# The last two pairs' sums by halves of the features, the final norm's root begun on ScalarE, and one product by the norm's weights on GpSimd

## The chip, the core and the metric

One core of a Trainium2 chip runs the whole program. A core has TensorE (PE: matrix products into PSUM, the banks `pb0` to `pb7`), VectorE (DVE), ScalarE (ACT), GpSimd (POOL) and SyncE (SP, which here only issues DMAs). The engines run their own instruction streams and meet at semaphores. The metric is the device time of one execution in microseconds (us), lower is better.

## The reference

A first block and a second block of a transformer work on 256 tokens of 1024 features in fp32, and what matters here is the very end of the second block: the hierarchical mixture of experts is added to the residual stream `h`, and one norm over the features follows.

```
def rms_norm(x, g):
    xf = x.astype(jnp.float32)
    y = xf * lax.rsqrt(jnp.mean(xf * xf, axis=-1, keepdims=True) + EPS)
    return (y * g.astype(jnp.float32)).astype(x.dtype)
...
    out = jnp.zeros_like(xn)
    for e in range(N_EXPERTS):
        hid = jax.nn.silu(xn @ w_gate[e]) * (xn @ w_up[e])
        out = out + (hid * cw[..., e:e + 1]) @ w_down[e]
    return out
...
        h = h + hierarchical_moe(rms_norm(h, ffn_norm_g[l]), w_router_group[l], b_router_group[l],
                                 w_router_expert[l], b_router_expert[l],
                                 w_exp_gate[l], w_exp_up[l], w_exp_down[l])
    return rms_norm(h, final_norm_g)
```

There are 32 experts of width 256, of which each token uses two. `EPS` is 1e-6.

## The kernel before

The tokens lie on the 128 partitions in two tiles (t = 0 and 1), the 1024 features beside each other, and a row of 1024 is worked in two halves (h = 0 and 1) of 512, because each PSUM tensor pb is 512 fp32 columns wide. `X` holds the residual stream; `half(X, t, h)` is one 128x512 quarter of it.

The expert stage (the function `sparse`) takes the experts in 16 pairs (`NP` = 16). For a pair p, PE gathers the tokens of the two experts, forms gate and up (line 2363), turns the hidden values (L2371), and multiplies by the down weights into banks 6 and 7 (L2386). ACT copies each half of that result to `YH` rounded to fp32r, the type in which PE multiplies here (L2472), and DVE writes the rest of it to `YL` (L2527). Then `pe_spread` (L2401) brings the pair's rows back to the tokens by a product with the selection matrix `SET`, once with `YH` and once with `YL`, and sums over all pairs in four banks: bank 2t + h for tile t and half h, so pb0 and pb1 belong to tile 0. Eight products a pair: two tiles, two halves, `YH` and `YL`. The eight of pair p - 2 stand in the middle of pair p. For the last two pairs they stand at the end, and the order is by tile: tile 0 of pair 14, tile 0 of pair 15, tile 1 of pair 14, tile 1 of pair 15. Each call of `pe_spread` first waits on the semaphore `yy_lo` for both halves of `YL` of its pair.

`finish` follows. DVE adds each bank to its quarter of `X` (L2551) in the order of (t, h) = (0,0), (0,1), then multiplies one half of tile 0 by the weights `FG` into `S1` (`with_gain`, L2544), and so on again with tile 1's adds and tile 0's other half. ACT squares each quarter and sums the squares (L2555; the sum comes by a second instruction, ACTIVATION_READ_ACCUMULATOR). DVE adds the two half sums of each tile (L2559) and takes the reciprocal root of the two values per partition in `dve_rsqrt` (L1476 to L1496): the value v, m = -v/2, a first guess by a shift and a subtraction on the bits, and three Newton steps, each of two TENSOR_SCALARs on one column (L1490) and one SCALAR_TENSOR_TENSOR (L1496). Then DVE forms tile 1's two halves, X times root times `FG` (L2564), while ACT scales tile 0's two products in `S1` by the root (L2569), and each of the four quarters of the output is stored by a DMA of its own (L2572), three from SP's queue and one from ACT's.

GpSimd does four small memsets of this kernel's own and nothing after 176 us. In the order listings below, pb, YH, YL and SET carry their buffer numbers; YH0/YL0 with SET2 are pair 14, YH1/YL1 with SET3 are pair 15. `s_rs`, `s_step_d`, `s_out_a` and so on are the semaphores; `s_step_d` orders DVE's small steps among themselves. S1 is the output buffer, NR and SM hold small per-partition values.

## Time and profile before

| | us |
|---|---|
| runs shown (3), median | 996.39 |
| lowest and highest | 995.97 and 996.99 |
| the profiled execution, device time | 997.38 |
| its span, first to last instruction | 995.5 |
| PE busy in the span | 970.2 (97%) |
| DVE / ACT / POOL busy | 543.4 / 476.7 / 0.8 |

The profile is of one execution; times in its rows are counted from the first instruction. It is read in three steps: the chain of waits tells what the end of the program hung on, the rows in order of time of one engine tell when each instruction began and how long it took, and the groups by line tell what an instruction of a kind costs. Two consecutive instructions of an engine may overlap by some hundredths of a microsecond, so the step from start to start is often shorter than the duration shown.

### The profile page before, as it was taken

To read this page: it belongs to the slowest core of one execution; us is meant where nothing else is said; L and a number is where in the kernel's file an instruction comes from. 1 tells how busy PE (TensorE), PEld (TensorE's weight loads), DVE (VectorE), ACT (ScalarE), POOL (GpSimd) and SP (SyncE) were. 2 spreads that over 40 slices of the span, in tenths; PEclk is the share of its full clock that TensorE was granted. 3 is DMA by queue.
4 is the path that set the end of the run, shared out by engine and by line. 5 is a ranking of instruction groups with operands and counts; after the bars stand their busy time and mean duration, and the time that the engine had idled before them with its cause. 6 is when DMAs were issued, how large, how long until landed. Compare 5 with 4: busy or idle time off the path is not lost.

```text
span 995.5 us, 13615 instructions
## 1 busy us (share of the span) xinstructions
PE 970.2 (97%) x5479; PEld 743.0 (75%) x5479; DVE 543.4 (55%) x875; ACT 476.7 (48%) x761; POOL 0.8 (0%) x8
## 2 busy tenths in 40 slices
PE   9999999898999999999999999999999999999995
PEld 8879877776889998888889887889874454455442
DVE  5888796655566646555586874676463112112114
ACT  5588555655346344543566656445443222222222
POOL 0000000000000000000000000000000000000000
PEclk9999999999999999999999999999999999999998
DMA  9934465522564555453645735375298999999993
GB/s 299 309 132 170 164 211 170 169 85 86 175 205 149 211 182 199 170 170 129 212 152 167 236 110 170 127 259 170 86 353 283 398 392 394 393 393 395 392 397 118
DMA packets 107268, 223.53 MB, mean 225 GB/s; under 512 B 10185, under 2 KB 15042, under 8 KB 107202
## 3 DMA queue, kind: packets, MB, share of 16 engines
q1 hardware_dynamic: 104752, 219.10, 62.5%
q10 hardware_dynamic: 2450, 3.51, 1.2%
q8 instruction: 46, 0.75, 0.3%
q14 instruction: 20, 0.16, 0.0%
HBM read 221.54 MB, written 1.05 MB: 224 GB/s over the span
## 4 chain that ended last, share of the span: by engine, by line
PE 80%; DVE 9%; ACT 5%; issue 3%; SPq 2%; DMA 1%; ACTq 0%; DVEq 0%
PE pb L461 16%; PE pb L463 16%; PE pb L462 16%; PE pb L2363 11%; PE pb L2386 6%; PE pb L2338 3%; DVE wl L1465 3%; PE pb L2401 3%; ACT wh L934 2%; PE pb L524 2%; DMA raw<-in_w_in 1%; SPq L429 1%; PE pb L595 1%; PE pb L664 1%; PE pb L2312 1%
## 5 line engine op out<-in xcount | busy, mean ns | idle before, releaser
L1465 DVE TENSOR_TENSOR wl<-raw,wh 128x2048 fp32r<-128x2048 f32 (+2 forms) x113 | 248.9, 2209 | 105.8 <-ACT wh L934 105.5
L934 ACT ACTIVATE wh<-raw 128x2048 fp32r<-128x2048 f32 (+2 forms) x114 | 208.3, 1835 | 113.2 <-PE pb L463 104.9
L461 PE MATMUL pb<-wh,th 128*128 128x512 f32 (+2 forms) x620 | 248.5, 401 | 1.3 <-DVE wl L1465 1.3
L463 PE MATMUL pb<-wh,tl 128*128 128x512 f32 (+2 forms) x620 | 242.1, 390 | 0.0
L462 PE MATMUL pb<-wl,th 128*128 128x512 f32 (+2 forms) x620 | 242.0, 390 | 0.0
L461 PE MATMUL pb<-th,wh 128*128 128x256 f32 x544 | 157.2, 289 | 0.2 <-DVE wl L1929 0.2
L463 PE MATMUL pb<-th,wl 128*128 128x256 f32 x544 | 154.1, 283 | 0.0
L462 PE MATMUL pb<-tl,wh 128*128 128x256 f32 x544 | 153.9, 283 | 0.0
L461 PEld LDWEIGHTS pb<-wh,th 128*128 128x128 f32 x620 | 117.1, 189 | 28.9 <-issue 4.1
L463 PEld LDWEIGHTS pb<-wh,tl 128*128 128x128 f32 x620 | 117.1, 189 | 25.7
L462 PEld LDWEIGHTS pb<-wl,th 128*128 128x128 f32 x620 | 117.2, 189 | 22.7
L461 PEld LDWEIGHTS pb<-th,wh 128*128 128x128 f32 x544 | 103.3, 190 | 3.7 <-issue 2.7
L462 PEld LDWEIGHTS pb<-tl,wh 128*128 128x128 f32 x544 | 103.4, 190 | 0.4
L463 PEld LDWEIGHTS pb<-th,wl 128*128 128x128 f32 x544 | 103.2, 190 | 0.0
L2519 DVE SCALAR_TENSOR_TENSOR S<-S,pb 128x256 f32<-128x256 f32 x16 | 6.7, 421 | 146.5 <-ACT S L2463 146.5
L2463 ACT ACTIVATE S<-pb 128x256 f32<-128x256 f32 x16 | 6.1, 383 | 98.2 <-PE pb L2363 98.2
L950 ACT ACTIVATE th<-pb,PC 128x256 fp32r<-128x256 f32 x61 | 25.0, 477 | 41.3 <-PE pb L524 41.3
L2446 ACT ACTIVATE XG<-pb,SM 128x256 f32<-128x256 f32 x64 | 26.6, 471 | 34.5 <-PE pb L2338 32.9
L2527 DVE TENSOR_TENSOR YL<-pb,YH 128x512 fp32r<-128x512 f32 x32 | 22.1, 692 | 34.7 <-ACT YH L2472 34.7
L2472 ACT ACTIVATE YH<-pb 128x512 fp32r<-128x512 f32 x32 | 19.1, 598 | 41.1 <-PE pb L2386 41.1
L2363 PE MATMUL pb<-raw,XG 128*64 128x512 f32 x160 | 36.1, 595 | 0.0
L1520 DVE SCALAR_TENSOR_TENSOR tl<-pb,PC,th 128x256 fp32r<-128x256 f32 x61 | 25.9, 477 | 18.7 <-ACT th L950 18.7
(372 smaller groups left out, 1088.4 us busy)
## 6 DMA issues: line engine op xcount, KB each, us to landing
raw<-in_w_in SPq DMA_DIRECT2D x31, 1024.0 KB, 5.7
raw<-in_w_up SPq DMA_DIRECT2D x16, 1024.0 KB, 6.1
raw<-in_w_down SPq DMA_DIRECT2D x16, 1024.0 KB, 4.9
raw<-in_w_exp_gate SPq DMA_DIRECT2D x20, 512.0 KB, 9.6
raw<-in_w_exp_up SPq DMA_DIRECT2D x20, 512.0 KB, 11.6
raw<-in_w_exp_down SPq DMA_DIRECT2D x10, 1024.0 KB, 13.8
raw<-in_w_xkv SPq DMA_DIRECT2D x8, 1024.0 KB, 5.0
mwh<-in_w_exp_gate SPq DMA_DIRECT2D x14, 512.0 KB, 10.3
```

The source lines that it names most:

```text
L461: PE.matmul(o, lh, rh, start=start, stop=False, skip_group_check=True)
L462: PE.matmul(o, lh, rl, start=False, stop=False, skip_group_check=True)
L463: return PE.matmul(o, ll, rh, start=False, stop=stop, skip_group_check=True)
L934: ACTE.activation(hi_of(i), raw_of(i), ACT.Copy).then_inc(S["hi"], 1)
L950: ACTE.activation(chunk(TH[which], c0 + c), PB[b][:, 0:256], ACT.Copy, scale=col(gain, c) if gain else scale).then_inc(S["turn_hi"], 1)
L1465: DVE.tensor_tensor(lo_of(i), raw_of(i), hi_of(i).bitcast(F), ALU.subtract).then_inc(S["lo"], 1)
L1520: DVE.scalar_tensor_tensor(chunk(TL[which], c0 + c), PB[banks[c % len(banks)]][:, 0:256], col(gain, c) if gain else scale, chunk(TH[which] ...
L2338: m = PE.matmul(b[:, 256 * k:256 * k + 256], l, s[:, t], start=(k == 0 and t == 0 and i == 0), stop=(t == 1 and i == 1), skip_group_check= ...
L2363: m = PE.matmul(b[64 * j:64 * j + 64, :].rearrange("p (g n) -> p g n", g=2), XG[q % 2][:, c + 64 * j:c + 64 * j + 64], w[:, :, j, k], star ...
L2386: m = PE.matmul(PB[6 + h][64 * j:64 * j + 64, :], HT[p % 2][:, 128 * k + 64 * j:128 * k + 64 * j + 64], w[:, j, 512 * h:512 * h + 512], st ...
L2401: m = PE.matmul(PB[2 * t + h][:, :], SET[p % 4][:, 128 * t:128 * t + 128], YY[p % 2][i][:, 512 * h:512 * h + 512], start=(p == 0 and i == ...
L2446: ACTE.activation(chunk(XG[q % 2], 2 * r + k), gather_bank(q, r)[:, 256 * k:256 * k + 256], ACT.Copy, scale=gffn[:, 2 * r + k:2 * r + k + ...
```

## The change

Four edits, all at the end of the expert branch:

1. `pe_spread` loses its argument for the tile. Pair 14 is spread whole (both tiles), and pair 15 by the new `pe_last_spread`: half 0 for both tiles, then half 1 for both tiles, each half behind a wait for its own half of `YL`, and with a signal behind each finished bank.
2. `finish` adds in the order (t, h) = (0,0), (1,0), (0,1), (1,1), one wait per bank, and ACT squares in that order. Tile 0's product by `FG` for half 0 is taken by GpSimd; the one for half 1 stays on DVE, behind all four adds. DVE's and ACT's last scalings both wait for these two products.
3. The root: ACT takes the square root of sum/1024 + EPS of both tiles (`act_seed`), DVE its reciprocal, and one Newton step follows in place of the bit trick and three steps (`dve_rsqrt_seeded`).
4. For it, ACT runs a square root on one column right behind the last pair's turned hidden values, and GpSimd writes EPS to a column at the start, for which DVE's first wait counts to 3.

```diff
@@ pool_main
             POOL.memset(ROW[:, :], 0.0).then_inc(S["zero"], 1)
+            POOL.memset(eps, EPS).then_inc(S["zero"], 1)
...
+        def act_seed(ss, n):
+            ACTE.activation(seed, ss, ACT.Sqrt, bias=eps, scale=1.0 / n).then_inc(S["root"], 1)
+
+        def dve_rsqrt_seeded(dst, ss, n):
+            v, y, t, m = NR[:, 0:2], NR[:, 40:42], NR[:, 80:82], NR[:, 20:22]
+            dve_then(DVE.tensor_scalar(v, ss, 1.0 / n, EPS, ALU.mult, ALU.add))
+            dve_after()
+            dve_then(DVE.tensor_scalar(m, v, -0.5, None, ALU.mult))
+            DVE.wait_ge(S["root"], 1)
+            dve_then(DVE.reciprocal(y, seed))
+            dve_after()
+            for c in range(2):
+                a, g = slice(c, c + 1), y[:, c:c + 1]
+                dve_then(DVE.tensor_scalar(t[:, a], m[:, a], g, g, ALU.mult, ALU.mult))
+            dve_after()
+            DVE.scalar_tensor_tensor(dst, t, 1.5, y, ALU.add, ALU.mult).then_inc(S["rs"], 1)
...
@@ dve_main
-            DVE.wait_ge(S["zero"], 2)
+            DVE.wait_ge(S["zero"], 3)
...
+            def pe_last_spread():
+                p = NP - 1
+                for h in range(2):
+                    PE.wait_ge(S["yy_lo"], 2 * p + h + 1)
+                    for t in range(2):
+                        for i in range(2):
...
+                        m.then_inc(S["spread"], 1)
...
-                for t in range(2):
-                    for p in (NP - 2, NP - 1):
-                        pe_spread(p, (t,))
+                pe_spread(NP - 2)
+                pe_last_spread()
...
@@ act_sparse
                         ACTE.activation(HT[p % 2], rise_bank(p)[:, 0:256], ACT.Copy).then_inc(S["ht"], 1)
+                        if p == NP - 1:
+                            ACTE.activation(seed[:, 0:1], eps, ACT.Sqrt).then_inc(S["const_r"], 1)
...
@@ finish
+            POOL.wait_ge(S["d_fing"], 16)
+            POOL.wait_ge(S["out_x"], 1)
+            POOL.tensor_tensor(half(S1, 0, 0), half(X, 0, 0), FG[:, 0:512], ALU.mult).then_inc(S["out_y"], 1)
+            DVE.wait_ge(S["d_fing"], 16)
+            DVE.wait_ge(S["out_x"], 3)
+            DVE.tensor_tensor(half(S1, 0, 1), half(X, 0, 1), FG[:, 512:1024], ALU.mult).then_inc(S["out_y"], 1)
...
-            dve_rsqrt(fr, [(f2, D)], last="rs")
+            f2_known = steps[0]
+            dve_rsqrt_seeded(fr, f2, D)
             DVE.wait_ge(S["rs"], len(SCALES) + 1)
+            DVE.wait_ge(S["out_y"], 2)
...
+            ACTE.wait_ge(S["step_d"], f2_known)
+            act_seed(f2, D)
             ACTE.wait_ge(S["rs"], len(SCALES) + 1)
+            ACTE.wait_ge(S["out_y"], 2)
             for h in range(2):
-                ACTE.wait_ge(S["out_y"], h + 1)
                 ACTE.activation(half(S1, 0, h), half(S1, 0, h), ACT.Copy, scale=fr[:, 0:1]).then_inc(S["out_a"], 1)
```

PE's last products before the change; the first column is the line, a wait stands in brackets:

```order
L2401 MATMUL pb1<-YL0,SET2 128x512
L2401 MATMUL pb0<-YH1,SET3 128x512 [waits s_yy_lo]
L2401 MATMUL pb0<-YL1,SET3 128x512
L2401 MATMUL pb1<-YH1,SET3 128x512
L2401 MATMUL pb1<-YL1,SET3 128x512
L2401 MATMUL pb2<-YH0,SET2 128x512 [waits s_yy_lo]
L2401 MATMUL pb2<-YL0,SET2 128x512
L2401 MATMUL pb3<-YH0,SET2 128x512
L2401 MATMUL pb3<-YL0,SET2 128x512
L2401 MATMUL pb2<-YH1,SET3 128x512 [waits s_yy_lo]
L2401 MATMUL pb2<-YL1,SET3 128x512
L2401 MATMUL pb3<-YH1,SET3 128x512
```

And with the change (L2422 is `pe_spread`, L2433 `pe_last_spread`):

```order
L2422 MATMUL pb1<-YL0,SET2 128x512
L2422 MATMUL pb2<-YH0,SET2 128x512
L2422 MATMUL pb2<-YL0,SET2 128x512
L2422 MATMUL pb3<-YH0,SET2 128x512
L2422 MATMUL pb3<-YL0,SET2 128x512
L2433 MATMUL pb0<-YH1,SET3 128x512 [waits s_yy_lo]
L2433 MATMUL pb0<-YL1,SET3 128x512
L2433 MATMUL pb2<-YH1,SET3 128x512
L2433 MATMUL pb2<-YL1,SET3 128x512
L2433 MATMUL pb1<-YH1,SET3 128x512 [waits s_yy_lo]
L2433 MATMUL pb1<-YL1,SET3 128x512
L2433 MATMUL pb3<-YH1,SET3 128x512
```

Pair 15's products of half 0 for both tiles now come before those of half 1, and all of pair 14 before them; before, the first product of pair 15 waited for both halves of its `YL`, now it waits for the first half, and only the products of half 1 wait for the second.

DVE at the end before the change, from the first add to the last scaling:

```order
L2551 TENSOR_TENSOR X<-X,pb 128x512 [waits s_spread,s_d_fing]
L2551 TENSOR_TENSOR X<-X,pb 128x512
L2544 TENSOR_TENSOR S<-X,FG 128x512 [waits s_out_x]
L2551 TENSOR_TENSOR X<-X,pb 128x512 [waits s_spread]
L2551 TENSOR_TENSOR X<-X,pb 128x512
L2544 TENSOR_TENSOR S<-X,FG 128x512 [waits s_out_x]
L2559 TENSOR_TENSOR NR<-NR 128x2 [waits s_out_a]
L1476 TENSOR_SCALAR NR<-NR 128x2 [waits s_step_d]
L1480 TENSOR_SCALAR NR<-NR 128x2 [waits s_step_d]
L1481 TENSOR_SCALAR NR<-NR 128x2
L1483 TENSOR_SCALAR NR<-NR 128x2 [waits s_step_d]
L1490 TENSOR_SCALAR NR<-NR 128x1 [waits s_step_d]
```

And with the change:

```order
L2578 TENSOR_TENSOR X<-X,pb 128x512 [waits s_spread] x4
L2590 TENSOR_TENSOR S<-X,FG 128x512 [waits s_out_x,s_d_fing]
L2593 TENSOR_TENSOR NR<-NR 128x2 [waits s_out_a]
L1511 TENSOR_SCALAR NR<-NR 128x2 [waits s_step_d]
L1513 TENSOR_SCALAR NR<-NR 128x2 [waits s_step_d]
L1515 RECIPROCAL NR<-SM 128x2 [waits s_root]
L1519 TENSOR_SCALAR NR<-NR 128x1 [waits s_step_d]
L1519 TENSOR_SCALAR NR<-NR 128x1
L1521 SCALAR_TENSOR_TENSOR NR<-NR 128x2 [waits s_step_d]
L2600 SCALAR_TENSOR_TENSOR S<-X,NR,FG 128x512 [waits s_out_y,s_rs]
```

One of DVE's two products by `FG` is gone and the other stands behind the adds; between the sum of the squares and the scaling there are six small instructions where there were thirteen.

ACT before the change, from the last turned hidden values on:

```order
L2483 ACTIVATE S<-pb 128x256 [waits s_used,s_ht_mm]
L2472 ACTIVATE YH<-pb 128x512 [waits s_spread,s_down_mm]
L2472 ACTIVATE YH<-pb 128x512 [waits s_spread,s_used]
L2555 ACTIVATE S,NR<-X 128x512 [waits s_out_x] x4
L2569 ACTIVATE S<-S,NR 128x512 [waits s_out_y,s_rs]
L2569 ACTIVATE S<-S,NR 128x512 [waits s_out_y]
```

And with the change:

```order
L2513 ACTIVATE S<-pb 128x256 [waits s_used,s_ht_mm]
L2515 ACT_TABLE_LOAD
L2515 ACTIVATE SM<-SM 128x1
L2502 ACTIVATE YH<-pb 128x512 [waits s_spread,s_down_mm]
L2502 ACTIVATE YH<-pb 128x512 [waits s_spread,s_used]
L2583 ACTIVATE S,NR<-X 128x512 [waits s_out_x] x4
L1506 ACTIVATE SM<-NR,SM 128x2 [waits s_step_d]
L2607 ACTIVATE S<-S,NR 128x512 [waits s_out_y,s_rs]
```

A table load and a square root of one column stand behind the turned hidden values, and one square root stands behind the four squares; no further table load stands in this branch.

GpSimd before the change has no instruction of its own in the expert branch. With it, from the memsets of the start on (L2587 is the product in `finish`):

```order
L1448 MEMSET RA 128x8x3
L1450 MEMSET BT 128x4x16 [waits s_turn_lo]
L2774 TENSOR_LOAD KW [waits s_flag]
L2782 COMPARE_AND_BRANCH
L2587 ISA
L2587 TENSOR_TENSOR S<-X,FG 128x512 [waits s_out_x,s_d_fing]
L2782 UNCONDITIONAL_BRANCH
```

## Rows read from the trace of the kernel before

**Rows 1.** By stretch: busy us of each engine (instructions), clock, DMA share, GB/s.

```profile
743.00:750.00 7.00, 6.21 (x38) 4.29 (x38) 6.70 (x18) 2.22 (x7) 0.00 (x0) 1.00 0.51 186
...
780.00:960.00 180.00, 180.00 (x922) 88.13 (x920) 34.80 (x84) 45.88 (x109) 0.00 (x0) 1.00 1.04 393
```

**Rows 2.** The chain that ended last, in order of time: start us, us, what.

```profile
981.16 0.70 DVE YL L2527
...
983.22 1.28 DVE X L2551 x2
...
987.11 0.17 DVE NR L2559
...
990.04 0.07 DVE S L2564
```

**Rows 3.** In order of time, PE: start us, us, engine, line, operation [idle before].

```profile
980.75 0.39 PE L2401 MATMUL pb<-YL,SET 128*128 128x512 f32 x1
980.98 0.39 PE L2401 MATMUL pb<-YH,SET 128*128 128x512 f32 x1
...
981.91 0.50 PE L2401 MATMUL pb<-YH,SET 128*128 128x512 f32 x1 [0.30 <-DVE YL L2527]
...
982.71 0.40 PE L2401 MATMUL pb<-YL,SET 128*128 128x512 f32 x1
```

**Rows 4.** In order of time, DVE, from the last pair to the root.

```profile
980.30 0.69 DVE L2527 TENSOR_TENSOR YL<-pb,YH 128x512 fp32r<-128x512 f32 x1 [4.27 <-ACT YH L2472]
...
984.42 0.69 DVE L2544 TENSOR_TENSOR S<-X,FG 128x512 f32<-128x512 f32 x1
...
987.30 0.17 DVE L1476 TENSOR_SCALAR NR<-NR 128x2 f32<-128x2 f32 x1
987.51 0.17 DVE L1480 TENSOR_SCALAR NR<-NR 128x2 f32<-128x2 f32 x1
...
987.98 0.46 DVE L1490 TENSOR_SCALAR NR<-NR 128x1 f32<-128x1 f32 x2
988.47 0.16 DVE L1496 SCALAR_TENSOR_TENSOR NR<-NR 128x2 f32<-128x2 f32 x1
```

**Rows 5.** In order of time, ACT, the last pair and the squares.

```profile
979.67 0.60 ACT L2472 ACTIVATE YH<-pb 128x512 fp32r<-128x512 f32 x1 [4.09 <-PE pb L2386]
...
983.95 0.63 ACT L2555 ACTIVATE S<-X 128x512 f32<-128x512 f32 x1 [2.82 <-DVE X L2551]
...
984.58 0.62 ACT L2555 ACTIVATE S<-X 128x512 f32<-128x512 f32 x1
...
986.37 0.61 ACT L2555 ACTIVATE S<-X 128x512 f32<-128x512 f32 x1
```

**Rows 6.** In order of time, all engines: a hand-over from DVE to ACT.

```profile
742.04 0.16 DVE L1880 TENSOR_TENSOR KW<-KW 128x8 f32<-128x8 f32 x1
742.22 0.20 ACT L1437 ACTIVATE KW<-KW 128x8 f32<-128x8 f32 x1
```

**Rows 7.** By line, ACT, shapes apart: busy us, mean ns, idle before.

```profile
L950 ACT ACTIVATE th<-pb,PC 128x256 fp32r<-128x256 f32 x61 | 25.0, 477 | 41.3 <-PE pb L524 41.3
...
L950 ACT ACTIVATE th<-pb 128x256 fp32r<-128x256 f32 x18 | 5.5, 389 | 12.0 <-PE pb L524 12.0
```

**Rows 8.** One line each, durations min/median/max in ns: L1782, then L1005.

```profile
L1782 DVE RECIPROCAL SM<-SM x4: 158/163/166, 687.7 to 707.7; 128x2 f32<-128x2 f32 x4
...
L1005 ACT ACT_TABLE_LOAD  x1: 1283/1283/1283, 98.3 to 98.3; - x1
```

**Rows 9.** In order of time, POOL at the start.

```profile
0.73 0.31 POOL L1444 MEMSET ROW<- 128x256 f32 x1 [0.29 <-POOLq L2755]
```

**Rows 10.** In order of time, PE weight loads: the last wait for a transfer.

```profile
972.60 0.32 PEld L2386 LDWEIGHTS pb<-BT,S 128*64 128x64 f32 x4 [0.54 <-DMA BT<-in_w_exp_down]
```

**Rows 11.** DMA issues: tensor, queue, KB each, us to landing; stretch 985 to 996.

```profile
out<-S SPq DMA_DIRECT2D x3, 256.0 KB, 2.9
```

**Rows 12.** The page, DMA issues of the whole span.

```profile
raw<-in_w_exp_gate SPq DMA_DIRECT2D x20, 512.0 KB, 9.6
```

More of the change, by code:

```diff
@@ L148 @@
      "sel", "cs_w", "ch_mm", "ch", "g_mm", "g_x", "rise_t", "rise_g", "over_mm", "ht_mm", "ht", "down_mm", "yy_hi", "yy_lo", "spread",
-     "xt_sum", "h_weighted", "out_x", "out_a", "out_y"])
+     "xt_sum", "h_weighted", "out_x", "out_a", "out_y", "root"])
 SEQ = S
@@ L270, in build @@
         rsx, hrsx = small(2), small(2)
+        eps, seed = small(1), small(2)
         hb, sp4, sp4n, sp8n = small(16), small(8), small(8), small(8)
@@ L2391, in pe_down, with pe_spread @@
                             m.then_inc(S["down_mm"], 1)
-            def pe_spread(p, tiles=(0, 1)):
+            def pe_spread(p):
                 PE.wait_ge(S["yy_lo"], 2 * p + 2)
@@ L2397, in pe_spread @@
                     PE.wait_ge(*gathered(0, 3))
-                for t in tiles:
+                for t in range(2):
                     for h in range(2):
@@ L2401, in pe_spread @@
                             m = PE.matmul(PB[2 * t + h][:, :], SET[p % 4][:, 128 * t:128 * t + 128], YY[p % 2][i][:, 512 * h:512 * h + 512],
-                                          start=(p == 0 and i == 0), stop=(p == NP - 1 and i == 1), skip_group_check=True)
-                if len(tiles) == 2 or p == NP - 1:
-                    m.then_inc(S["spread"], 1)
+                                          start=(p == 0 and i == 0), stop=False, skip_group_check=True)
+                m.then_inc(S["spread"], 1)
[3 more added lines that the diff above has]
+                    PE.wait_ge(S["yy_lo"], 2 * p + h + 1)
+                    for t in range(2):
+                        for i in range(2):
+                            m = PE.matmul(PB[2 * t + h][:, :], SET[p % 4][:, 128 * t:128 * t + 128], YY[p % 2][i][:, 512 * h:512 * h + 512],
+                                          start=False, stop=(i == 1), skip_group_check=True)
+                        m.then_inc(S["spread"], 1)
             def pe_sparse():
@@ L2533, in sparse @@
             dve_sparse()
-            finish(FG, [(S["spread"], NP - 1), (S["spread"], NP)])
+            finish(FG, [(S["spread"], NP + n) for n in range(4)])
         fs, fr, f2 = NR[:, 120:124], NR[:, 124:126], NR[:, 126:128]
         def finish(FG, done):
-            def with_gain(h):
-                DVE.wait_ge(S["out_x"], h + 1)
-                DVE.tensor_tensor(half(S1, 0, h), half(X, 0, h), FG[:, 512 * h:512 * h + 512], ALU.mult).then_inc(S["out_y"], 1)
-            DVE.wait_ge(S["d_fing"], 16)
-            for t in range(2):
-                DVE.wait_ge(*done[t])
-                for h in range(2):
+            for h in range(2):
+                for t in range(2):
+                    DVE.wait_ge(*done[2 * h + t])
                     o = half(X, t, h)
                     DVE.tensor_tensor(o, o, PB[2 * t + h][:, :], ALU.add).then_inc(S["out_x"], 1)
-                with_gain(t)
-            for j in range(4):
-                ACTE.wait_ge(S["out_x"], j + 1)
-                ACTE.activation(S0[:, 512 * j:512 * j + 512], half(X, j // 2, j % 2), ACT.Square,
-                                accum_out=fs[:, j:j + 1]).then_inc(S["out_a"], 1)
+            for n in range(4):
+                h, t = n // 2, n % 2
+                j = 2 * t + h
+                ACTE.wait_ge(S["out_x"], n + 1)
+                ACTE.activation(S0[:, 512 * j:512 * j + 512], half(X, t, h), ACT.Square,
+                                accum_out=fs[:, j:j + 1]).then_inc(S["out_a"], 1)
+            POOL.wait_ge(S["d_fing"], 16)
[4 more added lines that the diff above has]
+            DVE.tensor_tensor(half(S1, 0, 1), half(X, 0, 1), FG[:, 512:1024], ALU.mult).then_inc(S["out_y"], 1)
             s4 = fs.rearrange("p (t b) -> p t b", t=2)
@@ L2716, in dense @@
             dve_dense()
-            finish(FG, [(S["used"], NU)] * 2)
+            finish(FG, [(S["used"], NU)] * 4)
         early.close()
```

## Prediction

> **What bounds the kernel now.** I read the stretches first, then the chain of waits, then each engine in order of time. In the long expert stage PE is busy for all of 180 us from 780 to 960 while DVE and ACT work 35 and 46 us of it [rows 1]. So nothing that the change touches is worth anything before PE's last pair is done; it is the tail after it that can move. The chain runs there [rows 2] through DVE's second `YL` (981.16), PE's last spreads, the adds (983.22), the squares on ACT (the last at 986.37, [rows 5]), the sum of the squares (987.11) and DVE's small steps to the root, used at 990.04. From there to the end of the span at 995.5 lie the two scalings and the four stores; the change leaves these as they are, so what reaches 990.04 earlier ends the program earlier by as much. One figure is to be worked out: when is the root ready?
>
> **PE and the first add.** Now PE stops once: after four products it waits for the second `YL` and restarts at 981.91 [rows 3]. The products step by 0.23 us (980.75 to 980.98). With the change all eight of pair 14 run first, and by then `YL` of pair 15 is long there: its first half ends at 980.30 + 0.69 = 980.99 [rows 4], its second at 981.86 [rows 2]. So product n starts at 980.75 + (n - 2) x 0.233, and the stop (about 0.47 us against that step) is gone. But the first add does not wait for eight products any more, it waits for ten, since pair 14's tile 1 comes first: the tenth starts at 982.61. Today the eighth starts at 982.71 and the add 0.51 us later [rows 2, 3]; so the first add starts at 983.12, only **0.10 us** earlier. The next banks are finished by products 12, 14 and 16, ready for DVE at 983.59, 984.05 and 984.52.
>
> **The adds and squares.** Two adds take 1.20 us from start to start (983.22 to 984.42, [rows 2, 4]), 0.60 each. Four in a row start at 983.12, 983.72, 984.32 and 984.92; no bank is late for them, so the adds are DVE's pace. Before, a product by `FG` (0.69 us long, one more step of about 0.60) stood between adds two and three. ACT starts the first square 0.73 us after the first add's start (983.22 to 983.95) and steps by 0.63 (983.95 to 984.58) [rows 5]: 983.85, 984.48, 985.11, 985.74. The fourth add's result is there at 984.92 + 0.73 = 985.65, so ACT's own pace decides by a little. The sum of the squares starts 0.74 us after the last square's start (986.37 to 987.11), at **986.48** against 987.11: 0.63 us won. DVE's remaining product by `FG` starts at 984.92 + 0.60 = 985.52 and ends at 986.21, under ACT's last square, so it costs nothing; if that cover went, it would cost up to its 0.69.
>
> **The root.** Before: 987.11 to 990.04, 2.93 us [rows 2]. After, counted from the sum's start: the sum takes 0.16 and is followed by both ACT's square root and DVE's v. A hand-over of a small result from DVE to ACT costs 0.02 (742.04 + 0.16 to 742.22), and a small function takes 0.20 there [rows 6]. No row shows a square root of two columns whose bias is a column in memory; the nearest bound of what that column adds is 477 - 389 = 88 ns, the same instruction with and without a column as operand [rows 7]. I take 0.29; the ends are 0.20 and, were a table load to stand in front, 0.29 + 1.28 [rows 8]. So the square root is ready at 0.18 + 0.29 = 0.47, with a hand-over of 0.03 at 0.50. DVE's v starts at 0.19, m at 0.19 + 0.21 = 0.40 (987.30 to 987.51, [rows 4]), and m's step ends sooner than 0.50 allows, so ACT decides by a few hundredths. The reciprocal takes 0.16 (four rows of that shape, [rows 8]) plus 0.03 to the next dependent step: 0.69. The two column steps lead to the last step in 0.49 (987.98 to 988.47), which takes 0.16 + 0.03: **1.37 us**. The root is ready at 986.48 + 1.37 = 987.85, against 990.04.
>
> **The load of the tables and the small additions.** ACT's new table load and one-column root stand behind the last hidden values; 1.28 + 0.20 = 1.5 us, and ACT sits idle there for 4.09 us before 979.67 [rows 5]. It costs nothing; without that gap it would cost 1.5 us. The later squares and copies need no other load: the listing of ACT shows none. EPS in a column is one more small memset beside one of 0.31 us that starts at 0.73 us [rows 9], long before DVE's first use; it costs nothing for the same reason. On PE, DVE and ACT nothing else in the program moves; the late wait of both scalings for the two products of `FG` asks only that GpSimd is done.
>
> **The product on GpSimd.** The trace has no product there, only memsets. Its lower bound is DVE's own 0.69. From a memset of 256 columns in 0.31 [rows 9], 512 columns would be about 0.6 for a single stream, and three streams (two read, one written) one after the other some 1.4 to 1.8 us: my estimate is 1.4. It starts when the first add is done, about 983.12 + 0.70 = 983.82, and ends at about 985.2. It is needed at 987.85: a cover of 4.0 us. It costs nothing at either bound. The Trainium skill (GPSIMD Engine Reference, section Elementwise side-by-side cycle accounting) states 4497 ns for a product of this kind on 2048 columns; a quarter of that is an estimate of 1.1 us, and the sum would stay the same.
>
> **The sum.** 0.63 + (2.93 - 1.37) = 0.63 + 1.56 = 2.19 us. The profiled execution would go from a span of 995.5 to 993.3 and from 997.4 to 995.2; the median of the runs, 996.39, lies 1.0 below that execution, and the difference of the two kernels holds for both: **994.2 us**. That is 0.22%. A difference under 0.2% (2.0 us) is about what a measurement of this kernel cannot tell from none, so the forecast lies just beyond that line, and every tenth counts.
>
> **Rival 1: GpSimd and DVE get in each other's way.** GpSimd reads `X` and `FG` in just the time in which DVE does adds three and four. Nothing in the trace speaks for or against, since the two never work side by side there. If DVE's adds stood still while GpSimd works, the third add would start at 985.2 in place of 984.32, the fourth at 985.8, its square at 986.53 and the sum at 987.27: the 0.63 becomes -0.16, the gain 1.40 and the time 995.0. The Trainium skill (SBUF — State Buffer, the part on the shared port pair) says that a DVE instruction with two inputs in SBUF blocks and is blocked by one of GpSimd that reads SBUF, but not one with a single such input. By that rule the adds, whose other input is PSUM, are free, and only DVE's product would stand behind GpSimd's, from the point where that takes over 1.7 us (985.52 - 983.82); no run here shows it yet. Chance 0.14.
>
> **Rival 2: GpSimd's code is not there, slower than before.** The change brings the first real work on GpSimd, and with it a load of its code, at the head of the branch and without a wait in front. If this is done at once (about 744 us) it has 239 us of cover. It may add bytes to the weight stream, which fills the queues from 780 to 960 and at 972.60 keeps PE waiting 0.54 us [rows 1, 10]; but from 743 to 750 the queues are only half busy, so I count 0. If instead the code is fetched when the product is first run, at 983.9, the scalings wait for it. Everything is as before where fetch and product take 6.2 us (983.82 to 990.04), and the kernel is slower by over 0.2% from 8.2 us on. The price of a fetch is bounded by a 256 KB transfer on empty queues, 2.9 us [rows 11], and 512 KB on loaded ones, 9.6 us [rows 12]. With 2.9 + 1.4 the root waits 0.3 us (994.5); with 9.6 + 1.4 the end moves by 4.8 us, to 1001.2, and this is the rival. The listing has the load far in front, which speaks against it. The Trainium skill (GPSIMD Engine Reference, section Instruction dispatch) gives about 6 us for the first call after a load; were that paid at the product, by an estimate the time would be 997.6. Chance 0.05, of which 0.03 above 0.2%.
>
> **Rival 3: the steps are there but each costs a little more.** Hand-overs between ACT and DVE that are 0.05 to 0.1 longer, or a root of 0.4, cost 0.2 to 0.4 us: 994.4 to 994.6. That is the forecast's own case, on the other side of the line. I give forecast and this 0.78 together, split 0.57 beyond 0.2% and 0.21 within. That leaves 0.03 for things unseen, such as a further table load behind the first (1.28 us, time 995.5), all within 0.2%.
>
> **Chances and range.** Faster by over 0.2%: 0.57. Slower by over 0.2%: 0.03. Within: 0.21 + 0.14 + 0.02 + 0.03 = 0.40. The range goes from 993.3 (the sum is 0.3 us short, and the runs' own spread of half a microsecond) to 995.5, which takes in rival 1 and the table load; above it lies rival 2.
>
> **What will show it.** PE's last 16 products without a stop; the first add at about 983.1, no idle time between the four adds; the sum of the squares at about 986.5; a square root of about 0.29 us on ACT right behind it, no table load after 979; the scaling at about 987.9 and 1.4 us after the sum; GpSimd's product of 0.7 to 1.8 us beginning at 983.8. Adds that take longer than 0.69 us or that leave gaps would show rival 1; a scaling that waits for GpSimd, rival 2. The prediction is wrong if the tail after the root does not keep its 5.5 us.

## The result and the profile after

| | before | changed |
|---|---|---|
| median of 16 runs, us | 996.67 | 994.86 |
| lowest and highest | 995.64 and 998.36 | 993.17 and 996.83 |
| the profiled execution's span | 995.5 | 991.5 |
| in it: first of PE's last 16 spread products | 980.42 | 978.61 |
| in it: the root's first use | 990.04 | 985.96 |
| the tail between the two | 9.62 | 7.35 |

The ratio of the runs is 0.9977, with a 95% interval of 0.9970 to 0.9984: 2.3 us faster, or between 1.6 and 3.0. The medians differ by 1.8 us. The forecast of 994.2 us, 2.19 us faster, lies 0.7 us below the measured median and inside the interval of the difference; whether the gain passes 0.2% the interval leaves open.

The end of the chain of waits of the changed kernel, in order of time (start us, us, what), answers to [rows 2]:

```profile
978.68 2.06 PE pb L2422 x8
980.74 0.47 PE pb L2433 x2
...
981.24 0.70 DVE X L2578
...
981.96 2.57 ACT S L2583 x8
...
984.55 0.17 DVE NR L2593
...
985.96 0.07 DVE S L2600
```

PE's last products stand in it as one run without a stop, the four squares and their sums as one run of 2.57 us, and 1.41 us lie between the sum (984.55) and the root's use (985.96), where there were 2.93.

The same stretch of the changed kernel by instructions, in order of time, for DVE, ACT and GpSimd, answers to [rows 4, 5]:

```profile
981.24 2.48 DVE L2578 TENSOR_TENSOR X<-X,pb 128x512 f32<-128x512 f32 x4 [1.19 <-PE pb L2433]
...
981.96 0.63 ACT L2583 ACTIVATE S<-X 128x512 f32<-128x512 f32 x1 [2.63 <-DVE X L2578]
...
982.08 1.29 POOL L2587 TENSOR_TENSOR S<-X,FG 128x512 f32<-128x512 f32 x1 [806.36 <-DVE X L2578]
...
983.20 0.61 ACT L2583 ACTIVATE S<-X 128x512 f32<-128x512 f32 x1
983.64 0.68 DVE L2590 TENSOR_TENSOR S<-X,FG 128x512 f32<-128x512 f32 x1
...
983.81 0.61 ACT L2583 ACTIVATE S<-X 128x512 f32<-128x512 f32 x1
...
984.55 0.16 DVE L2593 TENSOR_TENSOR NR<-NR 128x2 f32<-128x2 f32 x1 [0.23 <-ACT S L2583]
...
984.75 0.30 ACT L1506 ACTIVATE SM<-NR,SM 128x2 f32<-128x2 f32 x1 [0.23 <-DVE NR L2593]
...
985.08 0.17 DVE L1515 RECIPROCAL NR<-SM 128x2 f32<-128x2 f32 x1
985.28 0.46 DVE L1519 TENSOR_SCALAR NR<-NR 128x1 f32<-128x1 f32 x2
985.77 0.16 DVE L1521 SCALAR_TENSOR_TENSOR NR<-NR 128x2 f32<-128x2 f32 x1
```

The four adds take 2.48 us as one run, in steps of 0.60; GpSimd's product works from 982.08 to 983.37 beside them; DVE's own product ends at 984.32, while ACT is still at its last square. The square root starts at the same time as DVE's v (984.75), takes 0.30 us, and the reciprocal follows 0.03 us behind it. And before it, the load of ACT's tables in its gap:

```profile
973.80 1.28 ACT L2515 ACT_TABLE_LOAD   x1
...
975.09 0.20 ACT L2515 ACTIVATE SM<-SM 128x1 f32<-128x1 f32 x1
...
977.87 0.60 ACT L2502 ACTIVATE YH<-pb 128x512 fp32r<-128x512 f32 x1 [2.58 <-PE pb L2407]
```

The load and the one-column root are over at 975.29, 2.58 us before ACT's next work, which answers to the 4.09 us of idle time in [rows 5].

One thing in the two spans is not of the change. The tail became 2.27 us shorter, the span 4.0. The other 1.8 us lie before the tail: PE's last products began at 978.61 in place of 980.42. The start of each of PE's 5479 products compared between the two traces shows where: the kernel before is 0.4 us behind from 127 us on (it leaves that for a few us around 184 and 208 and comes back), 1.9 from 234 us on, and stays between 1.7 and 1.95 behind from there to the tail (1.80 at its start). Between 229 and 233 us PE's granted clock was down in the one execution and not in the other. Rows by stretch, the columns as in [rows 1], of the kernel before:

```profile
229.00:231.00 2.00, 2.00 (x10) 1.71 (x10) 1.90 (x5) 1.61 (x3) 0.00 (x0) 0.65 0.96 374
```

and of the changed kernel:

```profile
229.00:231.00 2.00, 2.00 (x11) 1.67 (x10) 1.57 (x4) 1.97 (x3) 0.00 (x0) 1.00 1.05 409
```

The granted clock was 0.65 of full speed on average in one and full in the other. So what the change is worth is read from the tail, and the whole time is compared by many runs only.

### The profile page after: what moved, and what is told of

Same layout as the page of the kernel before. It is cut to its first block, busy times and chain, and to the rows that moved or that the text cites. A ratio compares the mean times of both kernels' runs of the same rounds, so it can differ in the third digit from the quotient of the medians.

```text
span 991.5 us, 13616 instructions
## 1 busy us (share of the span) xinstructions
PE 970.7 (98%) x5479; PEld 744.8 (75%) x5479; DVE 541.4 (55%) x867; ACT 478.0 (48%) x764; POOL 2.1 (0%) x10
## 4 chain that ended last, share of the span: by engine, by line
PE 81%; DVE 8%; ACT 5%; issue 3%; SPq 2%; DMA 1%; ACTq 0%; DVEq 0%
PE pb L462 17%; PE pb L464 16%; PE pb L463 16%; PE pb L2384 11%; PE pb L2407 6%; PE pb L2359 3%; PE pb L2422 3%; DVE wl L1467 3%; ACT wh L935 2%; PE pb L525 2%; PE pb L596 1%; SPq L430 1%; DMA raw<-in_w_in 1%; PE pb L665 1%; PE pb L2333 1%
```

## The experiments

All tails below are measured in the profiled execution of each kernel, from the first of PE's last 16 spread products to the first use of the root (start of DVE's first scaling), so what happened earlier in that execution does not enter. The time from there to the end of the span was 5.4 to 5.6 us in all twelve traces.

| kernel | expected tail | measured tail | of which up to the sum of the squares |
|---|---|---|---|
| before | | 9.62 | 6.69 |
| changed | 7.43 (forecast) | 7.35 | 5.94 |
| e1, root alone | 8.11 | 8.09 | 6.68 |
| e2, all but the root | 8.87 | 8.87 | 5.94 |
| e3, both products on DVE | 7.75 | 7.63 | 6.22 |
| e4, order by tiles | 8.1 | 8.09 | 6.68 |
| e5, 1024 columns on GpSimd | 7.35 or 8.5 | 8.30 | 6.02, and it stood for 1.03 |
| e6, no early load | 8.4 | 8.45 | 5.95 |
| e7, no Newton step | 6.66 | 6.74 | 5.95 |
| e8, half 0 first | 6.98 | 6.92 | 5.50 |
| e10, e8 and e7 | 6.3 | 6.30 | 5.50 |
| e11, e7 with v and m | 6.68 or 6.74 | 6.67 | 5.94 |

### e1: the new root alone

```diff
 (the kernel before)
-            dve_rsqrt(fr, [(f2, D)], last="rs")
+            f2_known = steps[0]
+            dve_rsqrt_seeded(fr, f2, D)
...
+            ACTE.wait_ge(S["step_d"], f2_known)
+            act_seed(f2, D)
```

> The kernel before with the new root alone (square root on ACT, reciprocal and one Newton step on DVE, table load behind the last hidden values); orders and products as before. Measure: the tail, from the first of PE's last 16 spread products to the first use of the root, 9.63 us before and 7.35 us with the whole change. Theory (the savings are separate steps of one chain and add up): the stretch from the sum of the squares to the use of the root is 1.41 us in place of 2.93, so the tail is 8.11 us and the time 1.5 us under the kernel before. Rival (what one part frees, the other would have hidden): less than 1.2 us won here.

Measured: the sum starts 6.68 us into the tail as before, the root is used 1.41 us behind it, the tail is 8.09. The time is 995.3 us, median of 12 runs, against 995.8 for 23 of the kernel before; ratio 0.9992 (0.9981 to 1.0004). The expected 0.9985 lies in that interval, which also holds no gain at all: the whole time alone would not have shown this step, the trace does. The rival of a hidden root falls.

### e2: everything but the root

```diff
-            f2_known = steps[0]
-            dve_rsqrt_seeded(fr, f2, D)
+            dve_rsqrt(fr, [(f2, D)], last="rs")
...
-            ACTE.wait_ge(S["step_d"], f2_known)
-            act_seed(f2, D)
...
-                        if p == NP - 1:
-                            ACTE.activation(seed[:, 0:1], eps, ACT.Sqrt).then_inc(S["const_r"], 1)
```

> The changed kernel with the old root (bit trick and three Newton steps on DVE, no square root and no table load on ACT); the new order of PE, adds and squares and the product on GpSimd stay. Theory (steps add up): the sum of the squares starts 5.94 us after the first spread product as in the changed kernel, the root takes 2.93 us, the tail is 8.87 us and the time about 0.7 us under the kernel before, which 5 rounds can hardly tell from none. Rival: if the order brings something only together with the new root, the tail is 9.4 us or more.

Measured: sum at 5.94, root 2.93 behind it, tail 8.87, all three as expected. Time 996.25 us against 995.8, ratio 1.0001 (0.9992 to 1.0011): the 0.75 us that the trace shows lie at the edge of what these runs can tell. 9.62 - 8.09 = 1.53 for the root and 9.62 - 8.87 = 0.75 for the rest make 2.28, and the whole change gave 2.27. The two parts add up; neither needs the other.

### e3: both products by the weights on DVE

```diff
-            POOL.wait_ge(S["d_fing"], 16)
-            POOL.wait_ge(S["out_x"], 1)
-            POOL.tensor_tensor(half(S1, 0, 0), half(X, 0, 0), FG[:, 0:512], ALU.mult).then_inc(S["out_y"], 1)
             DVE.wait_ge(S["d_fing"], 16)
             DVE.wait_ge(S["out_x"], 3)
+            DVE.tensor_tensor(half(S1, 0, 0), half(X, 0, 0), FG[:, 0:512], ALU.mult).then_inc(S["out_y"], 1)
```

> The changed kernel with both products by the norm's weights on DVE, behind the four adds; GpSimd does nothing at the end. Theory (GpSimd's part is to keep DVE free before the sum): the products start 5.03 and 5.63 us after the first spread product, the second ends at 6.32, the sum starts at 6.34 in place of 5.94 and the tail is 7.75 us, 0.4 more than with the change. Rival (GpSimd's product slows something that is now free of it): the adds or squares get shorter than 0.60 and 0.61 us a step, and the tail is under 7.6 us.

In order of time, DVE and ACT in e3:

```profile
983.35 0.68 DVE L2587 TENSOR_TENSOR S<-X,FG 128x512 f32<-128x512 f32 x1
...
983.95 0.68 DVE L2588 TENSOR_TENSOR S<-X,FG 128x512 f32<-128x512 f32 x1
984.05 0.19 ACT L2583 ACTIVATION_READ_ACCUMULATOR S<-X 128x1 f32 x1
984.55 0.15 DVE L2591 TENSOR_TENSOR NR<-NR 128x2 f32<-128x2 f32 x1
```

The second product starts at 983.95 and holds the sum of the squares, which ACT had ready at 984.24, until 984.55: 0.28 us later than in the changed kernel, not the 0.40 that I had expected (the second product let the sum start 0.60 behind its own start, where I had counted 0.71). Adds and squares keep their steps, so the rival falls. GpSimd's product is worth 0.28 us.

### e4: the order by tiles

```diff
-                pe_spread(NP - 2)
-                pe_last_spread()
+                for t in range(2):
+                    for p in (NP - 2, NP - 1):
+                        PE.wait_ge(S["yy_lo"], 2 * p + 2)
...
-            for h in range(2):
-                for t in range(2):
-                    DVE.wait_ge(*done[2 * h + t])
+            for t in range(2):
+                DVE.wait_ge(*done[t])
+                for h in range(2):
```

> The changed kernel with the order by tiles back, in PE's last spreads, the adds and the squares; GpSimd's product and the new root stay. Theory (the gain ahead of the root is that of the order): PE stops for the second remainder again, tile 1's banks are both finished only behind the 16th product, the third add starts 4.67 us after the first product, the sum at 6.7 and the tail is 8.1 us, 0.75 more than with the change. Rival (the gain ahead of the root comes from the product taken off DVE): the third add starts before 4.4 and the tail is under 7.7 us.

In order of time, DVE and GpSimd in e4 (the tail starts at 980.76):

```profile
983.48 1.28 DVE L2584 TENSOR_TENSOR X<-X,pb 128x512 f32<-128x512 f32 x2 [1.28 <-PE pb L2463]
...
984.32 1.29 POOL L2593 TENSOR_TENSOR S<-X,FG 128x512 f32<-128x512 f32 x1 [806.35 <-DVE X L2584]
...
985.35 1.29 DVE L2584 TENSOR_TENSOR X<-X,pb 128x512 f32<-128x512 f32 x2 [0.59 <-PE pb L2463]
...
987.44 0.16 DVE L2599 TENSOR_TENSOR NR<-NR 128x2 f32<-128x2 f32 x1 [0.20 <-ACT S L2589]
```

The third add starts 4.59 us into the tail, though DVE had been free since 984.76: it waits for tile 1's banks. The sum starts at 6.68, the place that it had before the change, with GpSimd's product in place and DVE relieved. So the product alone wins nothing. The order wins the 0.74 us ahead of the root, of which 0.28 depends on the product being off DVE.

e4 brings two things back at once, PE's stop and the finishing by tiles, and no run parts them. An estimate from rows of the changed kernel: with all of pair 14 first but pair 15 by tiles, tile 0's banks would both be finished by the 12th product (981.27, 2.66 us into the tail), the first add would start 0.43 behind it, and the sum 3.31 behind that as in the changed kernel, at 6.40. By this about 0.3 us of the 0.74 belong to the stop and somewhat over 0.4 to the order by halves.

### e5: the two engines side by side

```diff
-            POOL.wait_ge(S["out_x"], 1)
-            POOL.tensor_tensor(half(S1, 0, 0), half(X, 0, 0), FG[:, 0:512], ALU.mult).then_inc(S["out_y"], 1)
+            POOL.wait_ge(S["out_x"], 3)
+            POOL.tensor_tensor(S1[:, 0:1024], X[:, 0:1024], FG[:, 0:1024], ALU.mult).then_inc(S["out_y"], 2)
             DVE.wait_ge(S["d_fing"], 16)
-            DVE.wait_ge(S["out_x"], 3)
-            DVE.tensor_tensor(half(S1, 0, 1), half(X, 0, 1), FG[:, 512:1024], ALU.mult).then_inc(S["out_y"], 1)
```

> The changed kernel, but GpSimd takes both halves of tile 0 by the norm's weights in one product of 1024 columns behind the third add, and DVE none. GpSimd then works from about 4.6 to 7.1 us after the first spread product, while DVE does the small steps of the root, of which the sum of the squares and the last step read two inputs in SBUF. Theory A (the two engines do not hinder each other on these): the sum starts at 5.94 and the tail is 7.35 us, or as long as GpSimd needs if that is later. Theory B (an instruction of DVE with two SBUF inputs stands until GpSimd's is done): the sum starts only at about 7.1 and the tail is 8.5 us.

In order of time, GpSimd, ACT and DVE in e5:

```profile
985.69 2.34 POOL L2587 TENSOR_TENSOR S<-X,FG 128x1024 f32<-128x1024 f32 x1 [809.37 <-DVE X L2578]
...
986.73 0.19 ACT L2583 ACTIVATION_READ_ACCUMULATOR S<-X 128x1 f32 x1
987.02 1.03 DVE L2591 TENSOR_TENSOR NR<-NR 128x2 f32<-128x2 f32 x1 [0.91 <-ACT S L2583]
988.09 0.17 DVE L1511 TENSOR_SCALAR NR<-NR 128x2 f32<-128x2 f32 x1
```

DVE's sum of two pairs of numbers, 0.15 or 0.16 us long in every other trace, takes 1.03 us and ends at 988.05; GpSimd's product ends at 988.03. Theory B holds: an instruction of DVE that reads two inputs in SBUF stood until GpSimd was done. DVE's fourth add, which reads one input in SBUF and one in PSUM, began at about 985.4 and so ran on beside the product from 985.69; in the changed kernel adds two to four run beside GpSimd in their steps of 0.60. The Trainium skill (SBUF — State Buffer, Who interferes with whom) states that a DVE instruction with two SBUF inputs contends with a GpSimd instruction that reads SBUF, and one with at most one SBUF input does not; the measurement agrees. The tail is 0.95 us longer than with the change, in place of the 1.15 expected, since the sum ends when GpSimd is done, where I had counted it to start then. The sum's start is 0.08 us later than with the change (6.02 against 5.94); that has another cause, told under e7.

### e6: the table load where nothing hides it

```diff
-                        if p == NP - 1:
-                            ACTE.activation(seed[:, 0:1], eps, ACT.Sqrt).then_inc(S["const_r"], 1)
```

> The changed kernel without the one-column square root behind the last hidden values, so that the table load falls behind the four squares. Theory (the load costs its 1.28 us where nothing hides it, and starts when ACT's last square is read): the square root starts 1.06 us later than with the change, 7.2 us after the first spread product, and the tail is 8.4 us. Rival (a switch of tables costs more than the load shows): the tail is 9 us or more. Rival 2 (the load can run ahead of the squares): under 7.6 us.

In order of time, ACT and DVE in e6:

```profile
984.71 0.19 ACT L2581 ACTIVATION_READ_ACCUMULATOR S<-X 128x1 f32 x1
984.92 1.28 ACT L1506 ACT_TABLE_LOAD   x1
...
986.21 0.30 ACT L1506 ACTIVATE SM<-NR,SM 128x2 f32<-128x2 f32 x1
986.54 0.17 DVE L1515 RECIPROCAL NR<-SM 128x2 f32<-128x2 f32 x1 [1.04 <-ACT SM L1506]
```

The load starts 0.02 us behind ACT's read of the last sum and takes 1.28, the square root follows 0.01 later. The tail is 8.45, 1.10 more than with the change: less than the load's duration, since it starts beside DVE's sum of the squares and does not wait for it. So this load costs no more than its own duration; the Trainium skill (ScalarE: Activation LUTs, What ACT_TABLE_LOAD costs) adds a drain of 1380 ns to it, which this run does not show: between the read of the last sum (ended at 984.90) and the square root there is nothing but the load. Putting it behind the last hidden values kept 1.1 of the 1.5 us that the new root wins.

### e7 and e11: no Newton step

```diff
 (e7)
-            dve_then(DVE.tensor_scalar(v, ss, 1.0 / n, EPS, ALU.mult, ALU.add))
-            dve_after()
-            dve_then(DVE.tensor_scalar(m, v, -0.5, None, ALU.mult))
             DVE.wait_ge(S["root"], 1)
-            dve_then(DVE.reciprocal(y, seed))
-            dve_after()
-            for c in range(2):
...
-            dve_after()
-            DVE.scalar_tensor_tensor(dst, t, 1.5, y, ALU.add, ALU.mult).then_inc(S["rs"], 1)
+            DVE.reciprocal(dst, seed).then_inc(S["rs"], 1)
```

> The changed kernel without the Newton step: the root is the reciprocal of ACT's square root as it is, so the value of the norm is less exact. Theory (ACT's square root sets the start of the reciprocal, DVE's two preparing steps ran beside it): the reciprocal starts 0.53 us behind the sum of the squares as in the changed kernel, and the scaling 0.19 later, so the tail is 6.66 us, 0.69 less. Rival (the two preparing steps held the reciprocal back): it starts 0.1 or more earlier, tail under 6.6 us.

In order of time, e7:

```profile
985.26 0.30 ACT L1506 ACTIVATE SM<-NR,SM 128x2 f32<-128x2 f32 x1 [0.23 <-DVE NR L2583]
985.66 0.17 DVE L1511 RECIPROCAL NR<-SM 128x2 f32<-128x2 f32 x1 [0.44 <-ACT SM L1506]
```

The tail is 6.74, 0.61 less than with the change where 0.69 had been expected. The reciprocal starts 0.10 us behind the end of the square root, where it is 0.03 in the changed kernel. e11 keeps DVE's two preparing steps in front of it, though nothing uses them:

> e7_no_newton, but DVE still computes v and m, which nothing uses, between the sum of the squares and the reciprocal; the Newton step is left out. In e7 the reciprocal started 0.10 us behind the end of the square root, in the changed kernel 0.03. Theory A (the hand-over is quicker where DVE has just run another step): the reciprocal starts 0.53 us behind the sum, the tail is 6.68 us. Theory B (it is not, the 0.07 belongs to the way the two instructions meet in that run): 0.59, tail 6.74 us as in e7.

```profile
984.83 0.30 ACT L1506 ACTIVATE SM<-NR,SM 128x2 f32<-128x2 f32 x1 [0.23 <-DVE NR L2587]
...
985.03 0.17 DVE L1513 TENSOR_SCALAR NR<-NR 128x2 f32<-128x2 f32 x1
985.15 0.17 DVE L1515 RECIPROCAL NR<-SM 128x2 f32<-128x2 f32 x1
...
985.36 1.42 DVE L2594 SCALAR_TENSOR_TENSOR S<-X,NR,FG 128x512 f32<-128x512 f32 x2
```

The square root ends at 985.13, the reciprocal starts at 985.15, and the tail is 6.67. Two steps more on DVE made the chain 0.07 us shorter, the number of theory A. But that DVE had just run another step is not the reason: in e6 the hand-over was 0.03 too, after DVE had been idle for 1.04 us. The kernels differ in the waits in front of the reciprocal. In the changed kernel, e6 and e11, DVE's wait for the step before stands ahead of v, and the reciprocal has only the wait for the square root. In e7 and e10 v is gone, and both waits stand in front of the reciprocal. The chain of waits of e7 shows the wait for the square root (L1510) as a piece of its own on DVE's queue, between the end of the square root (985.56) and the reciprocal (985.66):

```profile
985.60 0.02 DVEq L1510
```

e10 has the same piece and 0.10 us. So has the sum of the squares in e5: its kernel leaves out DVE's product, so that the waits for `FG` and for the squares both stand in front of the sum, which starts 0.10 us behind ACT in place of 0.03:

```profile
986.96 0.02 DVEq L2590
```

In all of these, and in the first add of the kernel before (below), the wait that has the piece is the second in the code and the last to be met. The changed kernel's last scalings have two waits too, but there the one that is met last stands first, and they start 0.03 us behind the root without such a piece. That the order of two waits decides it fits every row; no run swaps them.

### e8 and e10: another order of the last products

```diff
 (e8)
-                pe_spread(NP - 2)
-                pe_last_spread()
+                two(a, 0, 0)
+                two(a, 0, 1)
+                PE.wait_ge(S["yy_lo"], 2 * b + 1)
+                two(b, 0, 0).then_inc(S["spread"], 1)
+                two(b, 0, 1).then_inc(S["spread"], 1)
+                two(a, 1, 0)
+                PE.wait_ge(S["yy_lo"], 2 * b + 2)
+                two(b, 1, 0).then_inc(S["spread"], 1)
+                two(a, 1, 1)
+                two(b, 1, 1).then_inc(S["spread"], 1)
```

`two(p, h, t)` stands for the two products of pair p, half h, tile t; a is pair 14, b pair 15.

> The changed kernel with another order of PE's last 16 products: pair 14 for half 0, pair 15 for half 0, then bank by bank for half 1, so that the four banks are finished behind products 6, 8, 12 and 16 in place of 10, 12, 14 and 16. Theory (after the change, the chain hangs on the first bank and four squares of 0.61 behind it; with earlier banks it hangs on the 16th product): the first add starts 1.7 us after the first product, the fourth at 4.1, the sum at 5.57, the tail is 6.98 us, 0.37 less than with the change and the time 2.6 us under the kernel before. Rival (the early banks collide with DVE's second remainder, or PE has to wait for it): no gain, tail 7.3 us or more.

In order of time, DVE and ACT in e8 (the tail starts at 978.93):

```profile
980.62 2.08 DVE L2596 TENSOR_TENSOR X<-X,pb 128x512 f32<-128x512 f32 x3 [0.25 <-PE pb L2440]
...
982.74 0.63 ACT L2601 ACTIVATE S<-X 128x512 f32<-128x512 f32 x1
982.96 0.69 DVE L2596 TENSOR_TENSOR X<-X,pb 128x512 f32<-128x512 f32 x1 [0.25 <-PE pb L2440]
...
983.68 0.63 ACT L2601 ACTIVATE S<-X 128x512 f32<-128x512 f32 x1 [0.22 <-DVE X L2596]
...
984.43 0.16 DVE L2611 TENSOR_TENSOR NR<-NR 128x2 f32<-128x2 f32 x1 [0.19 <-ACT S L2601]
```

The first add is 0.94 us earlier in the tail than with the change (1.69 against 2.63), but only 0.44 of it reach the sum (5.50 against 5.94): the chain now hangs on the 16th product, behind which the fourth add, its square and the sum must follow, and ACT waits 0.22 us for that add. The time is 993.21 us against 995.79, ratio 0.9975 (0.9964 to 0.9987), 12 runs against 17. The changed kernel's ratio was 0.9977, so only the tails show that e8 is the shorter of the two. e10 takes e8's order and e7's root:

> The order of PE's last products of e8_half_first together with e7_no_newton's root: reciprocal of ACT's square root without the Newton step, so the value is less exact. Theory (steps of one chain add up): the sum of the squares starts 5.50 us after the first spread product as in e8, the reciprocal 0.59 behind it and the scaling 0.20 later as in e7, so the tail is 6.3 us, 3.3 less than before, and the time about 3.3 us under the kernel before. Rival (something else is late once the root comes this early, GpSimd's product or DVE's other one by the norm's weights): a tail of 6.5 us or more, with a wait ahead of the scaling that does not end with the root.

Measured: sum at 5.50, reciprocal 0.60 behind, tail 6.30, time 993.42 us against 995.79, ratio 0.9974 (0.9965 to 0.9984). The trace puts it 3.3 us under the kernel before and 0.6 under e8; the times of the whole cannot tell it from e8 or from the changed kernel. As it drops the exact step for that, e8 is the version to keep: 0.43 us less tail than the change, with the same arithmetic in the root.

## Why the prediction was right

**The bound.** The tail was the place. PE is busy for all of 780 to 960 in the changed kernel too, and none of the edits reached further back.

**The first add.** Forecast 2.71 us into the tail, measured 2.63. The tenth product started 2.20 us into it, as counted; the add came 0.43 behind that, not 0.51. The term that was off is the hand-over: before, the first add waited for the weights `FG` as well, and with two waits in front of it the chain of the kernel before shows the one for the bank (L2548) as a piece of its own on DVE's queue, between PE's product and the add at 983.22:

```profile
983.16 0.02 DVEq L2548
```

With the change the wait for `FG` stands behind the adds. e1, which keeps it in front, has 0.50; e4, which moved it, has 0.43 with the old order. The prediction took 0.51 over from the kernel before although the wait had moved: 0.08 us.

PE's products at the border of the two pairs, in order of time, changed kernel:

```profile
980.34 0.40 PE L2422 MATMUL pb<-YL,SET 128*128 128x512 f32 x1
980.58 0.39 PE L2433 MATMUL pb<-YH,SET 128*128 128x512 f32 x1
980.81 0.39 PE L2433 MATMUL pb<-YL,SET 128*128 128x512 f32 x1
```

The steps are 0.24 and 0.23 us there too; the stop of [rows 3] is gone, as forecast.

**Adds and squares.** Steps of 0.60 and 0.61 to 0.63 as counted. Sum of the squares: forecast 6.07, measured 5.94; 0.08 of the 0.13 is that hand-over, the rest are squares of 0.61 where I had used 0.63.

**The root.** Forecast 1.37, measured 1.41. The square root took 0.30 (0.29 counted, from a small function and what an operand in memory adds, [rows 6, 7]); the reciprocal started 0.53 behind the sum in place of 0.50.

**The covers.** The table load was free, and e6 shows that without its gap it costs 1.10 us. DVE's product was free. GpSimd's product took 1.29 us (1.4 counted, between 0.69 and 1.8) and was done 2.6 us before it was needed.

**The sum.** 2.19 forecast, 2.27 measured in the tail, and 2.3 (1.6 to 3.0) in the ratio of the times. The part ahead of the root gave 0.75 where 0.63 was forecast, the root 1.52 where 1.56 was. The mechanism was the one forecast; that the sum is as close as 0.08 us owes a little to two errors of opposite sign.

**The rivals.** Rival 1, that GpSimd and DVE hinder each other, does not happen in this kernel (the adds keep their steps of 0.60), and is real as a mechanism: e5. DVE's product starts 0.27 us after GpSimd's has ended; a product of GpSimd that is 0.3 us longer would hold it, and from about 0.6 us longer (DVE's product has 0.3 us of room before the sum) the chain would feel it; these are estimates from the changed kernel's rows. Rival 2 does not happen: GpSimd starts its product 0.14 us after the first add's end (982.08 against 981.24 + 0.70), so no code is fetched then. The Trainium skill (GPSIMD Engine Reference, Instruction dispatch) states about 6 us for the first call of freshly loaded code; at the product, no such time is to be seen, and what the reload costs at the head of the branch is hidden, as PE's products of the two executions keep their distance from 234 us to the tail within 0.3 us. Rival 3, hand-overs that each cost more, does not happen: the first add's cost 0.08 less, and the reciprocal started 0.03 later than counted.

**The line of 0.2%.** I gave 0.57 to a gain beyond it. The tail says 0.23%, the ratio's interval reaches from 0.16% to 0.30%. A likely reason for so wide an interval stands in the last section.

## What to carry to other kernels

At the end of a kernel, where engines run one after another, read for each hand-over which instruction of the next engine could already start: letting PE run without its stop and finishing the banks in the order in which DVE takes them won 0.75 us here, of which 0.28 needs the product off DVE, and the better order of e8 another 0.43. A second engine's help counts only from the point where the first is late, which e3 and e4 put at 0.28 us and nothing, and GpSimd's help must not stand beside DVE instructions with two inputs in SBUF. A change of 2 us in 1000 is shown by the distance of two events in the trace, with one part undone at a time, long before the times show it.

## What the runs showed of the hardware that I had not expected

**The place of the clock's falls moves from run to run and is worth about as much as this change.** In each of the twelve traces TensorE's granted clock fell to half (1.2 of 2.4 GHz) for stretches of 3.4 us, one to three times between 126 and 230 us, and at no other place between the first microseconds and the tail. The kernel before had it at 209.1 and 229.6, the changed one at 183.7 and 207.6, e6 at 227.2 alone, e1 at 184.9, 208.7 and 229.2. PE had idled shortly before; in the kernel before, for 2.27 us ahead of the first row here. But the changed kernel has the same idle time there and no fall (second row), and e6 has one of 2.17 us ahead of 207.64 with no fall near it, and one of 2.28 ahead of 227.31, with its only fall (last two rows):

```profile
228.83 0.85 PE L595 MATMUL pb<-CT,S 128*128 128x128 f32 x6 [2.27 <-DVE RC L1616]
...
228.47 0.85 PE L596 MATMUL pb<-CT,S 128*128 128x128 f32 x6 [2.27 <-DVE RC L1637]
...
207.64 0.85 PE L596 MATMUL pb<-CT,RC 128*128 128x128 f32 x6 [2.17 <-DVE S L1637]
...
227.31 1.51 PE L596 MATMUL pb<-CT,S 128*128 128x128 f32 x6 [2.28 <-DVE RC L1637]
```

All twelve traces have these two idle stretches, of 2.15 to 2.28 us. So an idle stretch alone does not bring a fall; what else must be so is not shown.

What a fall costs can be read from such pairs of rows. From the product behind the first stretch to the one behind the second it is 21.15 to 21.21 us in the eight traces with a fall between 206.7 and 209.1 (21.17 in the kernel before), and 19.66 to 19.68 in the four without (e4, e6, e7, e11): 1.5 us. A fall at 227 to 230 costs 1.5 to 1.7 in the same way, and e4's at 126.9 costs 1.6. The falls at 183 to 185 of five traces cost nothing: the way from PE's product at 182 us to the one at 207 us is 25.5 us with and without. Six traces have two of the costly falls (before, e1, e2, e4, e5, e10) and begin the tail between 979.90 and 981.10 us; six have one (changed, e3, e6, e7, e8, e11) and begin it between 978.33 and 979.12. The kernels are the same up to the last of these falls but for a small memset and the places of small values in memory. One fall more or less is thus 1.5 us, and it is the larger part of the 1.8 us by which the two profiled executions differ ahead of the tail. The fastest and the slowest run of one kernel differ by 2.7 us (16 runs before) to 5.3 us (12 of e1), which makes the intervals as wide as they are; that the falls are behind it is inferred, as only profiled executions show where the clock fell.

**An instruction of DVE can be held for as long as GpSimd works**, and shows as one long instruction (1.03 for 0.16 us), not as idle time in front (e5).
